# A token-mixing layer's twelve gate projections, moved among attention and into its preparation

## The chip, the cores and the metric

The program runs on one core of one Trainium2 chip. The metric is the device time of one execution, in microseconds (us), and less is better.

## The reference

The program computes two transformer blocks of two layers each, all in float32, on 256 tokens of width 1024. The first block (retention and state-space branches, and a feed-forward) isn't touched. The second block works on the first one's result `x` and on a context `ctx` of 256 tokens. Its mixing, for each layer, is:

```python
z = h @ lp["w_in"]
cq, ckv, kr, zf, zp, zg = jnp.split(z, SPLITS, axis=-1)
q = _mla_q(cq, lp, ang)
k, v = _mla_kv(ckv, kr, lp, ang)
att = _latent_attention(q, k, v, kv_ctx)      # 8 heads, 512 keys: the context's 256 and x's 256
y_a = att @ lp["w_oa"]
y_b = _fourier_mix(zf) @ lp["w_ob"]
y_c = _pool_mix(zp, lp["w_grp"], lp["pool_scale"]) @ lp["w_oc"]
g = jax.nn.sigmoid(zg + lp["b_gate"])         # 3 gates of width 1024
g_a, g_b, g_c = jnp.split(g, 3, axis=-1)
return (g_a * y_a + g_b * y_b + g_c * y_c) @ lp["w_out"], (k, v)
```

Behind it, each layer has a part in which every token gathers 128 rows of a table (the "peer" part). The mixing runs three times: once for the context (layer 0), and twice for `x` (layers 0 and 1).

## The kernel before

A planner (`Plan`) writes one list of items by hand, and each engine's program goes through that list in its order and issues its own part of each item. So the list fixes the order on every engine, and an engine that waits holds all that stands behind it. Two generators are merged into the list: `x_stream` (the first block, then for each layer `mix_phase` and `peer_x`) and `context_stream` (the context's mixing and its peer part). A step that yields `"alone"` writes out what is left of the context stream before the list goes on.

The mixing is `mixer`. Its items for `x`, in their order:

- the preparation: `keys_values` in three steps (`low_rank` projection with `wkv` and `key_roped`; `low_turn`, which transposes the normalised rows on TensorE and scales them on VectorE at L1988; `kv_up` with `wukv`, L1561 and L1565), between its first two steps `low_rank` of the queries with `wcq`, then `low_turn` of the queries (transposes at L1333), and four `q_up` (96 rows at L1298, then the rotation at L1579).
- the attention: `attend` has 18 steps. Step i issues `att_out` of pair i-2 (products 64 wide at L1298), `att_turnp` of pair i-1 (transposes at L1333, which wait for ScalarE's exponential at L2402) and `att_score` of pair i (L1586). After eight heads an `att_turn` follows.
- `spectral`: the two items `fourier` and `pool`.
- twelve gates, `token_gate`: each is a product of a 1 MB weight `wzg` with `hT`, 16 products of 256 columns at L1298 (the trace has 32 records for them), and two tanh on ScalarE (L2421).
- four `mix`, each of three gates with the three branches, and four `token_out` with `wout`.

`beside(a, na, b, nb)` interleaves two generators evenly by their step counts. For `x` in layer 1 (`wide`) the two spectral items and the twelve gates stand beside the 18 attention steps, since twelve gate buffers have room there. For `x` in layer 0 only the two spectral items stand there, and the gates come behind attention, three ahead of each `mix`, in three buffers that lie on the preparation's memory. Weights are loaded through a ring of five 1 MB slots (`self.wx`) by SyncE's queue in the items' order: a load waits until the slot's last reader is done, and later loads stand behind it. PSUM banks are taken in rotation out of six.

Of the kernel before, what the change touches and what calls it, by code (L numbers as in the profile page):

```python
# [130 lines left out]
BIG_N = 53208  # L131
# [3 lines left out]
class Plan:  # L135
# [47 lines left out]
    def tick(self, name, by=1):  # L183

        self.counts[name] = self.counts.get(name, 0) + by
        return (self.sem(name), self.counts[name])

    def put(self, kind, **args):
        self.items.append((kind, args))
# [67 lines left out]

    def x_stream(self, ar):
        yield from self.first_block()
        for l in range(2):  # L260
            ar.at = self.xmark
            yield from self.mix_phase(self.px, Ring(self.wx), self.small, ar, l, self.X, 0, True)
            side = Arena(self.big, BIG_N - SIDE, SIDE)
            yield from self.peer_x(self.px, self.small, self.A0 + self.xmark, BIG_N - self.A0 - self.xmark - SIDE, l,
                                   self.X, iter(()) if l else self.context_keys(),
                                   [side.get(2048) for _ in range(3 if l else 4)], side if l else None)
# [554 lines left out]
    def mixer(self, banks, wr, sm, ar, l, hT, hT_ok, X, vec, rope_on, cs):  # L821
        put, tick, t = self.put, self.tick, self.t
# [3 lines left out]
            K, Vv = self.KC, self.VC  # L826
        attT = ar.get(1024, (4, 256))
        early = rope_on
        wide = rope_on and l == 1

        def mixed_buffers():
            return [ar.get(1024 if i == 1 else 512, (2, 512 if i == 1 else 256)) for i in range(6)]

        if early:
            zfT, AB, fT, zp, poT, pyT = mixed_buffers()
        sg_slots = [Slot(ar.get(512, (2, 256))) for _ in range(12)] if wide else None
        mark = ar.at
        kv = self.keys_values(banks, wr, sm, ar, l, hT, hT_ok, K, Vv, cs)
        yield next(kv)
        cqn, cqT = ar.get(512, (2, 256)), ar.get(512, (2, 256))  # L840
# [5 lines left out]
        w = self.load(wr, t["wcq"][l], 2048)  # L846
        made, scaled = self.low_rank(banks, sm, [w], w.ap.rearrange("p (k n) -> p k n", k=8), hT, None, 256, cqn)
        w.free(made)
        yield
        kv_ok = yield from kv  # L850
        if rope_on and l == 1:
            kv_ok += self.ctx_kv_ok
        turned = self.low_turn(banks, sm, 256, cqn, cqT, self.col[l, "qg"], scaled)
        yield 2
        w = self.load(wr, t["wuq"][l], 1536)
        wq = w.ap[:, 0:1536].rearrange("p (k n) -> p k n", k=2)
        for h in range(0, 8, 2):
            u = banks.take()
# [4 lines left out]
        w.free(u.full)  # L863

        nk = 4 if rope_on else 2
        got = {}

        def attend():
            state = {}
            pairs = [self.KC, K] if rope_on else [K]  # L870
            vals = [self.VC[:, 0, :], self.VC[:, 1, :]] + ([Vv[:, 0, :], Vv[:, 1, :]] if rope_on else [])
            if not rope_on:
                vals = [Vv[:, 0, :], Vv[:, 1, :]]
            for i in range(18):
                if i >= 2:
                    tt, h = divmod(i - 2, 8)
                    c, rc, pt, pt_ok = state.pop(i - 2)
                    u = banks.take()
                    pt.free(u.full)
                    put("att_out", pt=pt, vals=vals, h=h, nk=nk, u=u, ready=pt_ok, rc=rc, sm=sm, c=c,  # L880
                        dst=att[:, tt, 64 * h:64 * h + 64])
                    got["used", i - 2] = u.free
                    if h == 7:
                        ut = banks.take()
                        put("att_turn", src=att[:, tt, :], dst=attT[:, :, tt * P:tt * P + P], u=ut, ready=u.free)
                        got["aT"] = ut.free
                if 1 <= i < 17:
                    c, rc, p, e_ok = state.pop(i - 1)
                    pt, u = pts.take(), banks.take()
                    put("att_turnp", p=p, nk=nk, u=u, pt=pt, ready=e_ok)  # L890
                    p.free(u.full)
                    state[i - 1] = (c, rc, pt, u.free)
                if i < 16:
                    tt, h = divmod(i, 8)
                    u, p, c = banks.take(), prs.take(), 16 + 4 * (i % 4)
                    rc = tick("att_recip")
                    put("att_score", q=Q[:, h, tt * P:tt * P + P], pairs=pairs, h=h, nk=nk, u=u, p=p, sm=sm, c=c, rc=rc,
                        peak=tick("att_peak"), ready=[q_ok, *kv_ok] if i == 0 else [], before=got.get(("used", i - 4)))
                    state[i] = (c, rc, p, u.free)
                yield  # L900

        def spectral():
            w, u = self.load(wr, t["wzf"][l], 2048), banks.take()
            w.free(u.full)
            w2, ua = self.load(wr, t["dft"], 2048), [banks.take() for _ in range(2)]
            uf = banks.take()
            w2.free(uf.full)
            put("fourier", ws=[w, w2], u=u, ua=ua, uf=uf, hT=hT, zfT=zfT, AB=AB, fT=fT)
            got["f_ok"] = uf.free
            yield  # L910
            w, u = self.load(wr, t["wzp"][l], 2048), banks.take()
            w.free(u.full)
            w2, up = self.load(wr, t["pool"], 2048), banks.take()
            w2.free(up.full)
            w3, ug = self.load(wr, t["wgrp"][l], 256), banks.take()
            w3.free(ug.full)
            put("pool", ws=[w, w2, w3], u=u, up=up, ug=ug, hT=hT, zp=zp, poT=poT, pyT=pyT, psc=self.col[l, "psc"])
            got["py_ok"] = ug.free
            yield

        def gate(b, c, s):
            w, u = self.load(wr, t["wzg"][l, b, c], 2048), banks.take()
            w.free(u.full)
            n = 8 * b + 2 * c
            put("token_gate", ws=[w], u=u, hT=hT, s=s, bias=[self.col[l, "bg"][:, n + m:n + m + 1] for m in range(2)])
            return s, u.free

        def spectral_and_gates():
            yield from spectral()
            for c in range(4):  # L930
                for b in range(3):
                    got["gate", c, b] = gate(b, c, Turn(sg_slots[3 * c + b]))
                    yield

        if wide:
            yield from self.beside(spectral_and_gates(), 14, attend(), 18)
        elif early:
            yield from self.beside(spectral(), 2, attend(), 18)
        else:
            yield from attend()  # L940
        if not wide:
            ar.at = mark
            if not early:
                zfT, AB, fT, zp, poT, pyT = mixed_buffers()
                yield from spectral()
            sg_slots = [Slot(ar.get(512, (2, 256))) for _ in range(3)]
# [5 lines left out]
        for c in range(4):  # L952
            sgs = []
            for b in range(3):
                if wide:
                    sgs.append(got["gate", c, b])
                else:
                    sgs.append(gate(b, c, Turn(sg_slots[b])))
                    yield
            w, us = self.load(wr, t["woabc"][l, c], 2048), [banks.take() for _ in range(3)]  # L960
            w.free(us[2].full)
            for (s, _), u in zip(sgs, us):
                s.free(u.free)
            mixed = tick("mixed")
            put("mix", ws=[w], us=us, srcs=((attT, 0, 4), (fT, 4, 2), (pyT, 6, 2)), sgs=sgs, ty=ty,
                MT=MT[:, 2 * c:2 * c + 2, :], done=mixed, ready=[got["aT"], got["f_ok"], got["py_ok"]] if c == 0 else [])
            yield
        m2_ok = tick("d_m2_c" if vec else "d_m2_x", 16)
        put("load_row", dst=m2, src=self.mods[l, vec, 2:3, :].to_broadcast([P, 1024]), done=m2_ok, before=[got["aT"]])
        for i in range(4):  # L970
            w, u = self.load(wr, t["wout"][l, i], 2048), banks.take()
# [1758 lines left out]
```

## Time and profile before

| | us |
|---|---|
| median of 3 runs | 4190.04 (4188.73 to 4191.44) |
| the profiled execution | 4178.77 |
| its span | 4177.5 |
| mixing of `x` in layer 0, from the query projection to the output projection | 238.13 |
| the same in layer 1 | 217.21 |

The profiled execution was 11.27 us shorter than the median of the runs. The two stretches go from the start of the query `low_rank` on TensorE to the start of the first `token_out`; the work of TensorE in them is the same.

### The profile page before, as it was taken

To read this page: it belongs to the slowest core of one execution; us is meant where nothing else is said; L and a number is where in the kernel's file an instruction comes from. 1 tells how busy PE (TensorE), PEld (TensorE's weight loads), DVE (VectorE), ACT (ScalarE), POOL (GpSimd) and SP (SyncE) were. 2 spreads that over 40 slices of the span, in tenths; PEclk is the share of its full clock that TensorE was granted. 3 is DMA by queue.
4 is the path that set the end of the run, shared out by engine and by line. 5 is a ranking of instruction groups with operands and counts; after the bars stand their busy time and mean duration, and the time that the engine had idled before them with its cause. 6 is when DMAs were issued, how large, how long until landed. Compare 5 with 4: busy or idle time off the path is not lost. (4 is left out here: it accounts for less than half of the span.)

```text
span 4177.5 us, 41027 instructions
## 1 busy us (share of the span) xinstructions
PE 3664.8 (88%) x14584; PEld 2586.0 (62%) x14584; DVE 2318.4 (55%) x5464; ACT 656.9 (16%) x1800; POOL 1291.4 (31%) x1125
## 2 busy tenths in 40 slices
PE   8988999998998889999897998777778998887777
PEld 6667788887846778888745874333334786433333
DVE  3432011557757896766742147766764126777875
ACT  2332001110001320000012111111112211111111
POOL 1100000000655566765620014434442002444442
PEclk9999999999999999999999999988999999999989
DMA  8742344334998889998961449988996237999998
GB/s 320 283 193 88 122 151 181 122 130 150 411 390 308 296 334 397 404 392 343 413 238 53 145 186 389 412 340 359 415 416 281 102 116 295 385 419 420 419 419 332
DMA packets 207818, 1208.65 MB, mean 289 GB/s; under 512 B 23696, under 2 KB 24848, under 8 KB 96000
## 3 DMA queue, kind: packets, MB, share of 16 engines
q0 software_dynamic: 154368, 855.71, 51.1%
q1 hardware_dynamic: 53248, 350.32, 22.1%
q8 instruction: 118, 1.93, 0.2%
q14 instruction: 84, 0.69, 0.0%
HBM read 1204.79 MB, written 1.15 MB: 289 GB/s over the span
## 5 line engine op out<-in xcount | busy, mean ns | idle before, releaser
L1298 PE MATMUL bank<-big 128*128 128x256 f32 (+5 forms) x9848 | 2140.5, 378 | 64.1 <-DVE big L1796 8.7
L1298 PEld LDWEIGHTS bank<-big 128*128 128x128 f32 (+2 forms) x9848 | 1833.9, 191 | 377.9 <-issue 72.5
L2489 POOL DMA_INDIRECT big<-in_pboth,big x1024 | 1227.9, 1199 | 1208.1 <-PE bank L1685 705.2
L1685 PE MATMUL bank<-big 128*128 128x512 f32 x2048 | 1000.0, 647 | 276.6 <-ACT big L2453 276.6
L2169 DVE CUSTOM_DVE_ANT_0 big<-big 128x1024 f32<-128x1024 f32 x768 | 926.1, 1223 | 326.0 <-DMA big<-in_pboth,big 323.1
L1685 PEld LDWEIGHTS bank<-big 128*128 128x128 f32 x2048 | 413.4, 207 | 854.3 <-issue 492.6
L2476 POOL TENSOR_TENSOR big<-big 128x1 f32<-128x1 f32 (+1 forms) x49 | 37.7, 770 | 1519.8 <-DVE big L1739 1519.8
L2180 DVE SCALAR_TENSOR_TENSOR big<-big 128x1024 f32<-128x1024 f32 x254 | 326.2, 1284 | 61.5 <-DMA big<-in_pboth,big 41.5
L2453 ACT ACTIVATE big<-big 128x128 f32<-128x128 f32 x512 | 164.9, 391 | 244.0 <-DVE big L2148 239.7
L1333 PE MATMUL bank<-big 128*128 128x128 f32 x596 | 94.9, 294 | 66.0 <-ACT big L2402 19.8
L2443 ACT ACTIVATE big<-big 128x4 f32<-128x4 f32 (+2 forms) x134 | 27.7, 207 | 727.5 <-DVE big L2144 727.4
L1488 PE MATMUL bank<-big 128*128 128x512 f32 x256 | 113.9, 607 | 21.2 <-DVE big L1903 21.2
L1333 PEld LDWEIGHTS bank<-big 128*128 128x128 f32 x596 | 74.0, 153 | 84.4 <-issue 39.4
L2047 DVE SCALAR_TENSOR_TENSOR big<-big,bank 128x512 f32<-128x512 f32 x36 | 24.8, 689 | 176.1 <-PE bank L1298 176.1
L2025 DVE TENSOR_REDUCE big<-bank 128x1 f32<-128x512 f32 (+1 forms) x48 | 28.9, 602 | 152.8 <-PE bank L1586 152.8
L1812 DVE SCALAR_TENSOR_TENSOR big<-big,bank 128x512 f32<-128x512 f32 x32 | 22.0, 687 | 148.0 <-ACT big L2281 148.0
L1488 PEld LDWEIGHTS bank<-big 128*128 128x128 f32 x256 | 49.6, 195 | 84.7 <-issue 62.7
L1889 DVE SCALAR_TENSOR_TENSOR big<-big,bank 128x256 f32<-128x256 f32 x32 | 13.4, 420 | 152.7 <-PE bank L1298 152.6
L1796 DVE SCALAR_TENSOR_TENSOR big<-bank,big 128x255 f32<-128x255 f32 (+1 forms) x144 | 62.7, 477 | 61.4 <-ACT big L2269 59.7
L2238 ACT ACTIVATE big<-big 128x1024 f32<-128x1024 f32 x26 | 27.4, 1055 | 403.0 <-DVE big L1909 168.1
L2421 ACT ACTIVATE big<-bank,big 128x256 f32<-128x256 f32 x72 | 30.2, 471 | 305.2 <-PE bank L1298 305.2
L2482 POOL DMA_DIRECT2D big<-in_wmod x48 | 25.8, 540 | 153.8 <-PE bank L1510 153.8
(203 smaller groups left out, 2177.0 us busy)
## 6 DMA issues: line engine op xcount, KB each, us to landing
big<-in_w SPq DMA_DIRECT2D x104, 1024.0 KB, 7.6
big<-in_wmod POOLq DMA_DIRECT2D x48, 1024.0 KB, 8.4
big<-in_wgu SPq DMA_DIRECT2D x44, 1024.0 KB, 8.0
big<-in_wzg SPq DMA_DIRECT2D x36, 1024.0 KB, 4.7
big<-in_wro SPq DMA_DIRECT2D x32, 1024.0 KB, 6.9
big<-in_wpq SPq DMA_DIRECT2D x24, 1024.0 KB, 6.1
big<-in_wd SPq DMA_DIRECT2D x22, 1024.0 KB, 8.1
big<-in_pboth,big POOLq DMA_INDIRECT x1024, 11.7
```

What stands on the lines that cost most here:

```text
L1298: last = pe.matmul(o, a, b, start=(i == 0), stop=(i == n - 1))
L1333: last = pe.transpose(o[:, i, :], b, ident)
L1488: last = pe.matmul(us[2 * tt + n].ap, act[:, 2 * i + k, tt * P:tt * P + P], wk[:, k, 512 * n:512 * n + 512], start=(i + k == 0), stop=False)
L1685: last = pe.matmul(u.ap, d.ap, row[:, 512 * i:512 * i + 512], start=(k == 0), stop=(k == 127))
L1796: i = v.scalar_tensor_tensor(c[:, m, s:256], o[:, m, 0:256 - s], conv["w"][m][:, 3 - s:4 - s], c[:, m, s:256], ALU.mult, ALU.add)
L2025: step(v.reduce_max(sm[:, c:c + 1], u.ap[:, 0:nk * P], AX.X))
L2169: v.tensor_tensor_reduce(row, row, h, 1.0, 0.0, ALU.mult, ALU.add, out).then_inc(done[0], 1)
L2180: v.scalar_tensor_tensor(at, s.ap, by, at, ALU.mult, ALU.add).then_inc(done[0], 1)
L2421: last = e.activation(sc.ap[:, m, :], by2(u.ap)[:, m, :], ACT.Tanh, scale=0.5, bias=bias[m])
L2453: s.activation(d.ap, p.ident, ACT.Copy, scale=by).then_inc(diag[0], 1)
L2476: g.tensor_tensor(r.sm[:, 8 + r.at:8 + r.at + r.n], r.sm[:, 4 + r.at:4 + r.at + r.n], r.sm[:, 12:13].to_broadcast([P, r.n]), ALU.pow).then ...
L2489: g.indirect_dma_start(out=s.ap, out_offset=None, in_=table, in_offset=bass.IndirectOffsetOnAxis(ap=index, axis=0)).then_inc(s.full[0], 16)
```

## The change

For `x`, layer 0 takes the shape of layer 1: twelve gate buffers, here in the context stream's memory (free once the context's last item, `c_ok`, is done), and the gates in the list beside attention. In both layers the first three gates now stand in the preparation: one ahead of the keys' `low_turn`, one between that and `kv_up`, one between the queries' `low_turn` and `q_up`. The two spectral items come next, and the nine other gates, beside the 18 steps. The context's mixing keeps its order. In the list of items nothing moves ahead of the mixing of `x`: the context stream has already ended there, so that the new `"alone"` moves none of them.

```diff
     def x_stream(self, ar):
         yield from self.first_block()
+        yield "alone"
...
-        wide = rope_on and l == 1
+        wide = rope_on
...
-        sg_slots = [Slot(ar.get(512, (2, 256))) for _ in range(12)] if wide else None
+        if wide:
+            far = ar if l else Arena(self.big, self.B0, BIG_N - self.B0)
+            sg_slots = [Slot(far.get(512, (2, 256))) for _ in range(12)]
+            for s in sg_slots:
+                s.freed = self.c_ok
...
+        def spectral_and_gates():
+            for c in range(4):
+                for b in range(3):
+                    got["gate", c, b] = gate(b, c, Turn(sg_slots[3 * c + b]))
+                    yield
+                if c == 0:
+                    yield from spectral()
...
         yield
+        got = {}
+        fill = spectral_and_gates() if wide else iter(())
+        next(fill, None)
+        yield next(kv)
+        next(fill, None)
         kv_ok = yield from kv
...
         turned = self.low_turn(banks, sm, 256, cqn, cqT, self.col[l, "qg"], scaled)
+        next(fill, None)
         yield 2
...
-        def spectral_and_gates():
-            yield from spectral()
-            for c in range(4):
-                for b in range(3):
-                    got["gate", c, b] = gate(b, c, Turn(sg_slots[3 * c + b]))
-                    yield
-
         if wide:
-            yield from self.beside(spectral_and_gates(), 14, attend(), 18)
-        elif early:
-            yield from self.beside(spectral(), 2, attend(), 18)
+            yield from self.beside(fill, 11, attend(), 18)
         else:
             yield from attend()
```

The order on TensorE in the preparation, from the queries' `low_rank` (16 products of 256 columns) to the first `q_up` (96 wide). Before:

```order
L1298 MATMUL bank<-big 128x256 x16
L1333 MATMUL bank<-big 128x128 x2
L1561 MATMUL bank<-big 64x256 x8
L1565 MATMUL bank<-big 128x512 x2
L1333 MATMUL bank<-big 128x128 x4
L1298 MATMUL bank<-big 96x256 x4
```

And now (line numbers are higher by 10 in the changed kernel):

```order
L1308 MATMUL bank<-big 128x256 x32
L1343 MATMUL bank<-big 128x128 x2
L1308 MATMUL bank<-big 128x256 x16
L1571 MATMUL bank<-big 64x256 x8
L1575 MATMUL bank<-big 128x512 x2
L1343 MATMUL bank<-big 128x128 x4
L1308 MATMUL bank<-big 128x256 x16
L1308 MATMUL bank<-big 96x256 x4
```

Three gates (16 products of 256 columns each) have come in: one behind `low_rank` and one behind each of the two groups of transposes. Both layers have these rows.

The order on TensorE in layer 1's attention, from the end of `pool` (L1638) on; a step is `att_out` (64 wide), transposes, `att_score` (L1586). Before:

```order
L1638 MATMUL bank<-big 128x256 x2
L1298 MATMUL bank<-big 128x64 x4
L1333 MATMUL bank<-big 128x128 x4
L1586 MATMUL bank<-big 128x256 x2
L1298 MATMUL bank<-big 128x256 x16
L1298 MATMUL bank<-big 128x64 x4
L1333 MATMUL bank<-big 128x128 x4
L1586 MATMUL bank<-big 128x256 x2
L1298 MATMUL bank<-big 128x256 x16
L1298 MATMUL bank<-big 128x64 x4
L1333 MATMUL bank<-big 128x128 x4
L1586 MATMUL bank<-big 128x256 x2
```

And now, in both layers:

```order
L1648 MATMUL bank<-big 128x256 x2
L1308 MATMUL bank<-big 128x64 x4
L1343 MATMUL bank<-big 128x128 x4
L1596 MATMUL bank<-big 128x256 x2
L1308 MATMUL bank<-big 128x64 x4
L1343 MATMUL bank<-big 128x128 x4
L1596 MATMUL bank<-big 128x256 x2
L1308 MATMUL bank<-big 128x256 x16
L1308 MATMUL bank<-big 128x64 x4
L1343 MATMUL bank<-big 128x128 x4
L1596 MATMUL bank<-big 128x256 x2
L1308 MATMUL bank<-big 128x64 x4
```

Of the first steps behind `pool`, layer 1 had a gate ahead of each; now the third step has none, the fourth has one and the fifth has none. In steps 3 to 15 ten gates stood before in layer 1 and seven stand now.

The end of layer 0's mixing on TensorE before, from the last attention steps to the output projection (20 groups of 16: twelve gates, four `mix`, four `token_out`):

```order
L1298 MATMUL bank<-big 128x64 x4
L1333 MATMUL bank<-big 128x128 x4
L1298 MATMUL bank<-big 128x256 x320
L1343 MATMUL bank<-big 128x256 x10
```

And now:

```order
L1308 MATMUL bank<-big 128x64 x4
L1343 MATMUL bank<-big 128x128 x4
L1308 MATMUL bank<-big 128x256 x128
L1353 MATMUL bank<-big 128x256 x10
```

The twelve gates have left this place (192 products).

## Rows read from the trace of the kernel before

**Rows 1.** The core's span and granted TensorE clock.

```profile
core 0: 4177.5 us, clock 0.951
```

**Rows 2.** Windows of both mixings of x: length, busy us by engine, clock, DMA.

```profile
core 0: us, PE busy (x) PEld busy (x) DVE busy (x) ACT busy (x) POOL busy (x), PEclk, DMA share, GB/s
2188.70:2426.80 238.10, 210.60 (x983) 171.90 (x981) 44.39 (x94) 46.69 (x108) 0.70 (x1) 0.95 0.29 104
3216.20:3433.50 217.30, 200.21 (x984) 166.55 (x983) 44.37 (x94) 47.58 (x108) 0.69 (x1) 0.98 0.32 114
```

**Rows 3.** TensorE's timeline, starts of query projection and output projection: start, us, work, [idle].

```profile
2188.70 7.10 PE L1298 MATMUL bank<-big 128*128 128x256 f32 x32
...
2426.83 28.00 PE L1298 MATMUL bank<-big 128*128 128x256 f32 x128 [1.60 <-DVE big L2052]
...
3216.25 7.10 PE L1298 MATMUL bank<-big 128*128 128x256 f32 x32
...
3433.46 28.00 PE L1298 MATMUL bank<-big 128*128 128x256 f32 x128 [1.61 <-DVE big L2052]
```

**Rows 4.** TensorE's timeline, layer 1's preparation.

```profile
3223.19 0.38 PE L1333 MATMUL bank<-big 128*128 128x128 f32 x2
3224.99 3.67 PE L1561 MATMUL bank<-big 128*64 128x256 f32 x16 [1.43 <-DVE big L1988]
...
3230.41 0.60 PE L1333 MATMUL bank<-big 128*128 128x128 f32 x4
3232.11 1.94 PE L1298 MATMUL bank<-big 128*96 128x256 f32 x8 [1.10 <-DVE big L1988]
...
3245.52 1.07 PE L1579 MATMUL bank<-big 96*96 96x512 f32 x2 [0.76 <-ACT big L2381]
3248.90 2.05 PE L1586 MATMUL bank<-big 96*128 96x256 f32 x4 [2.31 <-issue]
```

**Rows 5.** TensorE's timeline, layer 1's attention.

```profile
3283.01 1.03 PE L1586 MATMUL bank<-big 96*128 96x256 f32 x4
...
3292.09 1.03 PE L1586 MATMUL bank<-big 96*128 96x256 f32 x4
...
3331.92 1.03 PE L1586 MATMUL bank<-big 96*128 96x256 f32 x4
...
3335.16 1.06 PE L1333 MATMUL bank<-big 128*128 128x128 f32 x8 [1.17 <-ACT big L2386]
3336.06 1.03 PE L1586 MATMUL bank<-big 96*128 96x256 f32 x4
...
3384.97 1.03 PE L1586 MATMUL bank<-big 96*128 96x256 f32 x4
...
3402.54 0.63 PE L1333 MATMUL bank<-big 128*128 128x128 f32 x4 [0.56 <-ACT big L2386]
```

**Rows 6.** TensorE's timeline, layer 0: two attention steps without a gate, gates and mix.

```profile
2259.49 0.63 PE L1333 MATMUL bank<-big 128*128 128x128 f32 x4 [0.97 <-ACT big L2402]
...
2262.99 0.63 PE L1333 MATMUL bank<-big 128*128 128x128 f32 x4 [0.97 <-ACT big L2402]
...
2329.73 95.50 PE L1298 MATMUL bank<-big 128*128 128x256 f32 x440
```

**Rows 7.** Windows at the start of attention: layer 0, layer 0 further on, layer 1.

```profile
2219.00:2241.00 22.00, 17.13 (x54) 14.10 (x54) 6.01 (x15) 5.38 (x13) 0.00 (x0) 0.54 0.00 0
2241.00:2286.00 45.00, 35.44 (x197) 27.67 (x197) 9.45 (x26) 15.12 (x37) 0.00 (x0) 1.00 0.14 48
3247.00:3255.00 8.00, 6.10 (x14) 4.90 (x15) 2.71 (x6) 0.78 (x2) 0.00 (x0) 0.57 0.00 0
```

**Rows 8.** DMA issues of layer 1's mixing: count, KB each, median us to landing.

```profile
big<-in_wzg SPq DMA_DIRECT2D x6, 1024.0 KB, 4.8
...
big<-in_wzf SPq DMA_DIRECT2D x1, 1024.0 KB, 10.9
```

**Rows 9.** Timeline: the context's last addition on VectorE; a gate's tanh pair on ScalarE.

```profile
2139.59 2.36 DVE L2202 TENSOR_TENSOR big<-big 128x1024 f32<-128x1024 f32 x2
...
3291.01 0.84 ACT L2421 ACTIVATE big<-bank,big 128x256 f32<-128x256 f32 x2 [5.18 <-PE bank L1298]
```

More of the change, by code:

```diff
@@ L835, in mixer, with spectral, gate @@
             zfT, AB, fT, zp, poT, pyT = mixed_buffers()
-        sg_slots = [Slot(ar.get(512, (2, 256))) for _ in range(12)] if wide else None
-        mark = ar.at
+        if wide:
[3 more added lines that the diff above has]
+                s.freed = self.c_ok
+        mark = ar.at
+        def spectral():
+            w, u = self.load(wr, t["wzf"][l], 2048), banks.take()
+            w.free(u.full)
+            w2, ua = self.load(wr, t["dft"], 2048), [banks.take() for _ in range(2)]
+            uf = banks.take()
+            w2.free(uf.full)
+            put("fourier", ws=[w, w2], u=u, ua=ua, uf=uf, hT=hT, zfT=zfT, AB=AB, fT=fT)
+            got["f_ok"] = uf.free
+            yield
+            w, u = self.load(wr, t["wzp"][l], 2048), banks.take()
+            w.free(u.full)
+            w2, up = self.load(wr, t["pool"], 2048), banks.take()
+            w2.free(up.full)
+            w3, ug = self.load(wr, t["wgrp"][l], 256), banks.take()
+            w3.free(ug.full)
+            put("pool", ws=[w, w2, w3], u=u, up=up, ug=ug, hT=hT, zp=zp, poT=poT, pyT=pyT, psc=self.col[l, "psc"])
+            got["py_ok"] = ug.free
+            yield
+        def gate(b, c, s):
+            w, u = self.load(wr, t["wzg"][l, b, c], 2048), banks.take()
+            w.free(u.full)
+            n = 8 * b + 2 * c
+            put("token_gate", ws=[w], u=u, hT=hT, s=s, bias=[self.col[l, "bg"][:, n + m:n + m + 1] for m in range(2)])
+            return s, u.free
+        def spectral_and_gates():
+            for c in range(4):
+                for b in range(3):
+                    got["gate", c, b] = gate(b, c, Turn(sg_slots[3 * c + b]))
+                    yield
+                if c == 0:
+                    yield from spectral()
         kv = self.keys_values(banks, wr, sm, ar, l, hT, hT_ok, K, Vv, cs)
@@ L865, in mixer @@
         nk = 4 if rope_on else 2
-        got = {}
         def attend():
@@ L900, in attend @@
                 yield
[L902 to L909, printed above, removed]
-            yield
[L911 to L926, printed above, removed]
-        def spectral_and_gates():
-            yield from spectral()
-            for c in range(4):
-                for b in range(3):
-                    got["gate", c, b] = gate(b, c, Turn(sg_slots[3 * c + b]))
-                    yield
         if wide:
-            yield from self.beside(spectral_and_gates(), 14, attend(), 18)
-        elif early:
-            yield from self.beside(spectral(), 2, attend(), 18)
+            yield from self.beside(fill, 11, attend(), 18)
         else:
             yield from attend()
+        if not wide or l == 0:
+            ar.at = mark
         if not wide:
-            ar.at = mark
             if not early:
```

## The prediction

> **What bounds the kernel now.** I first read the windows over both mixings of `x` [rows 2]. TensorE is busy for 210.60 of 238.10 us in layer 0 and 200.21 of 217.30 in layer 1, ScalarE and VectorE under 48 each, the DMA queues at 0.29 and 0.32. TensorE sets the time here (its clock is granted at 0.951 over the whole span of 4177.5 us [rows 1]); what can be gained is its idle time and its time at the low clock. Both stretches hold the same work. By the starts of query and output projection [rows 3], layer 0 takes 2426.83 - 2188.70 = 238.13 us and layer 1 3433.46 - 3216.25 = 217.21. So the two orders of the gates have already run side by side in one execution, and the order of layer 1 is 20.92 us shorter.
>
> Where these 20.92 us lie: a gate in a dense stream costs 32 x 95.50/440 = 6.95 us [rows 6] wherever there is no gap to fill. An attention step without a gate repeats every 2262.99 - 2259.49 = 3.50 us: its transposes wait 0.97 us for the exponential [rows 6]. A step with a gate takes 3292.09 - 3283.01 = 9.08 us [rows 5]. So a gate put into a step costs 9.08 - 3.50 = 5.58, which is 1.37 less than in the stream (0.97 of wait and 0.4 of the pipe's draining and refilling). Ten or eleven gates covering such a gap give about 14 us. The rest is the clock: layer 0's attention starts with 22 us at a mean of 0.54 of the full 2.4 GHz, that is 20.2 us at 1.2 GHz; layer 1 shows 0.57 over 8 us, that is 6.9 us [rows 7]. Half of the difference is 6.7 us. 14 + 6.7 is close to 20.92, so I hold the difference explained.
>
> **The change, term by term.**
>
> *Layer 0 takes layer 1's old order*: -20.92 us, as measured between the layers. The stretch has the same dependences, the same ring and the same weights in both; only the bank numbers and the place of the buffers differ.
>
> *Three gates enter the preparation, in both layers.* They add 3 x 6.95 = 20.85 us there. The first stands ahead of the keys' transposes, which follow the query projection without any idle time (3216.25 + 7.10, next start 3223.19) [rows 3, 4]: it covers nothing. The second stands between those two transposes and `kv_up`. From 3223.19 to 3224.99 is 1.80 us, of which two transposes in a stream take 0.22 (four take some 0.45); 1.58 us go. The third stands between the queries' four transposes and `q_up`: 3232.11 - 3230.41 = 1.70, less 0.45, gives 1.25 us. The idle times alone, 1.43 and 1.10, would give 2.53, my lower bound for what is covered; I take 1.58 + 1.25 = 2.83, since the drain is covered as well. Net +18.02. The gaps of 0.76 between the four `q_up` and of 2.31 ahead of the first score [rows 4] stay.
>
> *The same gates leave the attention.* In steps 3 to 15 the old layer 1 has ten gates and three steps without one, of which one is the step with `att_turn`, 3336.06 - 3331.92 = 4.14 us [rows 5]: 10 x 9.08 + 2 x 3.50 + 4.14 = 101.94, and the trace has 3384.97 - 3283.01 = 101.96. By the new order there are seven gates and six plain steps, and one of the gates now stands in the step with `att_turn`. That combination is not in the trace at that place. I price it as 9.08 + 0.45 for four more transposes + 0.56 idle as where `att_turn` follows a gate at the end of attention [rows 5] + 0.17 of overlap lost in that wait = 10.26 (bounds 9.53, no wait, and 10.7, the full 1.17 of the row at 3335.16). So 6 x 9.08 + 10.26 + 6 x 3.50 = 85.74, which is 16.22 less. The two last steps keep their gates.
>
> *Sum of the moved three*: +18.02 - 16.22 = +1.80 us in each layer: taken out of the attention they saved 5.58 each, in the preparation they cost 6.95 each, less only two small gaps. With the bounds 2.53 and 3.2 for the gaps, and those of the `att_turn` step, it is +0.7 to +2.6. Layer 0: -20.92 + 1.80 = -19.12. Layer 1: +1.80. Together -17.3.
>
> *What could wait instead.* Loads: a gate's weight lands 4.8 us after its issue when it is alone, and the last of five issued together after 10.9 [rows 8]. Of the first five loads now three are the two gates' and `wukv` instead of `wukv`, `wuq` and `wzf`, about 4 MB either way; the first gate's product starts some 24 us after the issue. `wuq` has to wait for the slot of `wcq`, free when the query projection ends, and is needed three gates (20.8 us) and `kv_up` later; `wzf`, `dft`, `wzp` and `pool` follow in the queue as the gates and `kv_up` release their slots, each over 14 us ahead of its use. All are covered by TensorE's own products; without that cover each would cost up to 4.8 us. ScalarE: each gate puts 0.84 us of tanh [rows 9] ahead of the copies of K or Q. The first of four heads' K takes TensorE about as long, and the first `q_up` 1.94 us [rows 4]: nothing shows, at most 0.84 a gate. The gate buffers of layer 0 wait on ScalarE for the context's last item, which ended at 2141.95 [rows 9]; the first tanh stands at about 2188.70 + 14 = 2203, 61 us later.
>
> **The clock** is what I cannot price from one row. In both layers it falls to 1.2 GHz around the 2.31 us of idle that follow four `q_up` with gaps between them, and comes back inside `fourier` [rows 4, 7]. In layer 1 this costs about 6.9/2, less the idle part, some 3 us. The change leaves this sequence as it is, so I leave the 3 us in both layers. The Trainium skill says, in "TensorE: Matmul & The Clock Gate" (Part 1: The HAM clock gate), that the low clock is the default and that activity releases it; by that a denser preparation may hold the clock, and the sum would be up to 6 us lower. The trace agrees so far that the falls come with idle time; whether the gates ahead of `q_up` are enough no row shows.
>
> **Sum.** The profiled execution would go from 4178.77 to 4161.5 us. It stood 11.27 us under the median of the runs; I see nothing in the mixings that explains it, so I put the same -17.3 on the median: 4190.04 - 17.3 = 4172.7 us.
>
> **Rivals.**
>
> 1. *The sum holds* (layer 0 like layer 1, the clock's fall as in layer 1): 4172.7, own range 4170 to 4176. Chance 0.63. For it: the two orders lie in one trace, and every other stretch keeps its order.
> 2. *The clock doesn't fall at the start of attention*, in one layer or both, because the third gate stands just ahead of `q_up`: 3 or 6 us less, 4169.7 or 4166.7. Against it: the idle stretch itself, 2.31 us behind thin work, is unchanged. Chance 0.20.
> 3. *The clock stays low for longer*, as in layer 0 before (20.2 us instead of 6.9 at 1.2 GHz, 6.7 us a layer): 4179. For it: six plain steps instead of three with idle time in each; against it: a row of plain steps of layer 0 ran at 1.00 [rows 7]. Chance 0.06.
> 4. *The change doesn't shorten the program*, as layer 0's mixing isn't what the rest waits for: the peer part behind it would start no earlier, and the time stays at 4190 to 4194. Against it: the output projection follows its work with 1.60 us of idle only [rows 3], and everything of the peer part starts from its result. Chance 0.06.
> 5. *Slower*: the tanh of the first gate is behind the context's last item on ScalarE, and all of ScalarE behind that tanh. If the context stream ended late, layer 0's whole preparation would stall. It decides from a delay of 61 us on, where the wait begins, and at 61 + 17 = 78 us nothing is left; at 90 us later the kernel would take about 4202. The rows show the context done 61 us ahead, and nothing that the change moves lies ahead of it. Chance 0.03.
>
> A remainder of 0.02 is for what I don't see.
>
> **Numbers.** A measurement of this kernel can tell about 0.2%, 8.4 us, from no change. Rivals 1 to 3 all lie more than that below 4190.04: with the margin of the sum, 0.91 for faster, 0.06 for no difference, 0.03 for slower. The range of 8 in 10 takes in rivals 1 and 2 whole and most of 3: 4165 to 4179.
>
> **What would show it.** In the profile of the changed kernel: from query projection to output projection, now with one gate more ahead of the keys' transposes, both layers about 219 us. No idle ahead of `kv_up` and the first `q_up`. Six plain steps with 0.97 us of idle ahead of their transposes between steps 3 and 15, and a wait for L2386's counterpart of about 0.56 at the `att_turn` in the middle. The half clock for some 7 us at the start of each attention. I am wrong if the layers differ by more than 4 us, if a DMA or a bank appears among TensorE's waits of these stretches, or if a stretch outside the mixings changes its length by more than 2 us.

## The result and the profile after

| | before | after |
|---|---|---|
| median, us (7 runs each) | 4189.67 (4184.69 to 4192.37) | 4175.02 (4172.86 to 4179.59) |
| ratio, 95% interval | | 0.9967 (0.9956 to 0.9978) |
| the profiled execution, us | 4178.77 | 4172.86 |
| mixing of `x`, layer 0, us | 238.13 | 220.85 |
| mixing of `x`, layer 1, us | 217.21 | 217.58 |
| between the mixings, us | 789.42 | 794.65 |
| behind the second mixing, us | 744.04 | 750.24 |

The changed kernel is 14.65 us faster by the medians; the forecast was 17.3. The whole interval lies below 1, on the side of faster. The two mixings together became 17.28 - 0.37 = 16.91 us shorter. The two profiled executions differ by 5.91 us only, because the stretches outside the mixings, whose code did not change, were 11.4 us longer in the second one.

TensorE's timeline of the changed kernel in layer 1: start, length, line, work, [idle before, what ended it].

```profile
3203.78 14.03 PE L1308 MATMUL bank<-big 128*128 128x256 f32 x64
3217.65 0.38 PE L1343 MATMUL bank<-big 128*128 128x128 f32 x2
3217.87 7.10 PE L1308 MATMUL bank<-big 128*128 128x256 f32 x32
3224.90 3.67 PE L1571 MATMUL bank<-big 128*64 128x256 f32 x16
...
3230.32 0.60 PE L1343 MATMUL bank<-big 128*128 128x128 f32 x4
3230.75 8.83 PE L1308 MATMUL bank<-big 128*128 128x256 f32 x40
...
3254.43 1.83 PE L1596 MATMUL bank<-big 96*128 96x256 f32 x4 [2.32 <-issue]
3256.06 8.09 PE L1308 MATMUL bank<-big 128*128 128x256 f32 x32
...
3287.20 1.03 PE L1596 MATMUL bank<-big 96*128 96x256 f32 x4
...
3290.17 0.63 PE L1343 MATMUL bank<-big 128*128 128x128 f32 x4 [0.96 <-ACT big L2412]
...
3334.23 1.07 PE L1343 MATMUL bank<-big 128*128 128x128 f32 x8 [0.56 <-ACT big L2396]
...
3421.36 28.00 PE L1308 MATMUL bank<-big 128*128 128x256 f32 x128 [1.61 <-DVE big L2062]
```

The first row holds the query projection and a gate without a gap. The idle times of 1.43 and 1.10 us of [rows 4] are gone: `kv_up` (L1571) and the first `q_up` (the last 8 of the 40 records at 3230.75) follow a gate at once. The 2.32 us ahead of the first score have stayed. In the attention plain steps wait 0.96 or 0.97 us, and the step with `att_turn` (L1343 x8) waits 0.56 us instead of the 1.17 of [rows 5].

The same timeline in layer 0, around what layer 1 doesn't have:

```profile
2238.93 2.05 PE L1596 MATMUL bank<-big 96*128 96x256 f32 x4 [2.31 <-issue]
2240.77 8.84 PE L1308 MATMUL bank<-big 128*128 128x256 f32 x32
...
2285.18 1.03 PE L1596 MATMUL bank<-big 96*128 96x256 f32 x4
2286.17 1.08 PE L1308 MATMUL bank<-big 128*128 128x64 f32 x8
2288.56 0.99 PE L1343 MATMUL bank<-big 128*128 128x128 f32 x4 [1.32 <-ACT big L2412]
...
2409.13 28.00 PE L1308 MATMUL bank<-big 128*128 128x256 f32 x128 [1.61 <-DVE big L2062]
```

One plain step waits 1.32 us for the exponential instead of 0.97 (what was late is in the last section), and behind it four transposes take 0.99 us instead of 0.63. For these and for the long first rows the windows of the changed kernel tell why (length, busy by engine, then the granted clock, here 0.77, 0.76 and 0.87, and DMA):

```profile
2235.00:2250.00 15.00, 11.75 (x38) 8.87 (x38) 3.25 (x7) 1.53 (x4) 0.00 (x0) 0.77 0.03 9
2285.00:2292.00 7.00, 5.68 (x27) 4.65 (x25) 1.64 (x4) 2.47 (x7) 0.00 (x0) 0.76 0.45 153
3251.00:3264.00 13.00, 10.64 (x38) 8.16 (x38) 2.98 (x6) 0.78 (x2) 0.00 (x0) 0.87 0.03 10
```

TensorE ran at 1.2 GHz for 6.9 us at the start of layer 0's attention, for 3.4 us at the start of layer 1's, and once more for 3.4 us in layer 0 around that longer wait.

### The profile page after: what moved, and what is told of

The parts are those of the page before. It is cut to its first block and busy times, and to the rows that moved or that the text cites. A ratio compares the mean times of both kernels' runs of the same rounds, so it can differ in the third digit from the quotient of the medians.

```text
span 4171.6 us, 41042 instructions
## 1 busy us (share of the span) xinstructions
PE 3669.1 (88%) x14584; PEld 2587.9 (62%) x14584; DVE 2321.4 (56%) x5464; ACT 657.2 (16%) x1800; POOL 1283.5 (31%) x1125
## 5 line engine op out<-in xcount | busy, mean ns | idle before, releaser
L1343 PE MATMUL bank<-big 128*128 128x128 f32 x596 | 95.5, 296 | 64.0 <-ACT big L2310 20.6
L2035 DVE TENSOR_REDUCE big<-bank 128x1 f32<-128x512 f32 (+1 forms) x48 | 28.9, 603 | 173.6 <-PE bank L1596 173.6
L1343 PEld LDWEIGHTS bank<-big 128*128 128x128 f32 x596 | 75.0, 154 | 81.4 <-issue 35.0
```

The lines of the kernel that those rows point to most:

```text
L1343: last = pe.transpose(o[:, i, :], b, ident)
L2035: step(v.reduce_max(sm[:, c:c + 1], u.ap[:, 0:nk * P], AX.X))
```

## The experiments

All mixings below are cut at the same four points of TensorE's timeline: P, from the query projection to the first score; F, with `fourier` and `pool`, to the third score (step 2); S, the thirteen steps to the score of step 15; E, from there to the output projection. The table is worked out from the timeline of each profile, in us.

| kernel | layer | P | F | S | E | sum |
|---|---|---|---|---|---|---|
| before | 0 | 32.66 | | | | 238.13 |
| before | 1 | 32.65 | 34.11 | 101.96 | 48.49 | 217.21 |
| changed | 0 | 50.65 | 33.74 | 87.97 | 48.49 | 220.85 |
| changed | 1 | 50.65 | 32.77 | 85.67 | 48.49 | 217.58 |
| changed, third execution | 0 | 50.66 | 31.09 | 86.30 | 48.48 | 216.53 |
| shape_only | 0 | 32.65 | 34.16 | 102.32 | 48.48 | 217.61 |
| shape_only | 1 | 32.65 | 31.10 | 103.63 | 48.49 | 215.87 |
| two_gaps | 0 | 43.72 | 33.79 | 92.39 | 48.49 | 218.39 |
| two_gaps | 1 | 43.72 | 32.77 | 92.40 | 48.49 | 217.38 |
| behind_q_up | 0 | 48.18 | 31.02 | 86.30 | 48.48 | 213.98 |
| behind_q_up | 1 | 48.18 | 31.01 | 85.67 | 48.49 | 213.35 |
| one_behind_q_up | 0 | 37.12 | 31.02 | 96.84 | 48.49 | 213.47 |
| one_behind_q_up | 1 | 37.11 | 31.02 | 98.88 | 48.49 | 215.50 |
| gap_and_behind | 0, 1 | 42.55 | 31.02 | 90.72 | 48.49 | 212.78, 212.77 |
| q_up_staggered | 0 | 38.77 | 31.02 | 90.72 | 48.49 | 209.00 |
| q_up_staggered | 1 | 38.77 | 31.02 | 92.39 | 48.49 | 210.67 |

The second execution of the changed kernel repeats each cell of its two rows within 0.02 us. At full clock F is 31.02 us.

Theory 1 is that of the prediction: a product in the stream costs what it takes, one in a plain attention step 1.37 us less, the gain is layer 0's shape, and the three moved gates cost a little. Its rivals stand with each run. Every ratio is to the kernel before, measured beside the run on the same chip.

### Both kernels once more

> The kernel before, unchanged, for its profile alone. In the two profiles so far the stretch between the mixings (first output projection to the query projection of layer 1) went from 789.4 us before to 794.7 after, and the stretch behind the second mixing from 744.0 to 750.2, together 11.4 us longer, while the two mixings became 16.9 us shorter. Theory 1 (the profiled execution of before was a short one; the peer part varies by itself): here one or both stretches come out longer, 792 to 798 and 747 to 752, and the mixings at 238.1 and 217.2 as before within 2 us. Rival (the change lengthens the peer part): 789.4 and 744.0 again within 1.5 us.

> The changed kernel, unchanged. Mixing stretches 220.8 and 217.6 us again within 3 us (clock at the start of attention differs from execution to execution); ratio to before about 0.9967. Theory 1: the stretch between the mixings and the one behind differ from 794.7 and 750.2 by 1 to 5 us. Rival: they come out as 794.7 and 750.2 within 1.5.

Windows from output projection to the next query projection, and from the second output projection to the end: the kernel before, first execution, and below it the second one.

```profile
2426.80:3216.20 789.40, 628.29 (x1680) 314.64 (x1681) 522.81 (x1480) 133.03 (x419) 296.57 (x264) 0.93 0.89 362
3433.50:4177.50 744.00, 599.91 (x1508) 292.04 (x1508) 517.66 (x1454) 116.19 (x380) 284.83 (x260) 0.92 0.92 379
```

```profile
2427.20:3224.30 797.10, 643.41 (x1681) 321.43 (x1682) 523.20 (x1480) 133.19 (x419) 297.44 (x264) 0.91 0.89 359
3441.30:4189.50 748.20, 598.52 (x1508) 292.30 (x1508) 517.80 (x1454) 116.20 (x380) 287.92 (x260) 0.93 0.92 377
```

The same kernel took 797.1 and 748.2 us in its second profile, 11.9 more than in the first, with the same instructions to within a record; its mixings were 237.81 and 217.01. (TensorE was granted 0.91 instead of 0.93 and busy for 15.1 us more in the longer first stretch, but 0.93 instead of 0.92 in the second, which was longer too; why these stretches vary stays open.) That settles it for theory 1: the first profile of before was a short one. The changed kernel's repeat gave 797.27 and 749.04, and mixings of 220.83 and 217.59. In all 13 profiles the first stretch lies between 787.2 and 800.7 us and the second between 744.0 and 750.2; the kernel before has 789.4 and 797.0 in the first, the changed one 794.7, 797.3 and 794.8, so no effect of the gates' order can be told there. The repeat's median was 4169.85 us beside 4186.62 for the kernel before, its ratio 0.9955 (0.9942 to 0.9969).

### Layer 0's shape alone

The three `next(fill, None)` of the preparation are left out, and `spectral` comes ahead of the first gate:

```diff
+                    if 3 * c + b == 0:
+                        yield from spectral()
...
-                if c == 0:
-                    yield from spectral()
...
-        next(fill, None)
         yield next(kv)
-        next(fill, None)
         kv_ok = yield from kv
...
-        next(fill, None)
         yield 2
...
-            yield from self.beside(fill, 11, attend(), 18)
+            yield from self.beside(fill, 14, attend(), 18)
```

> Layer 0 in layer 1's old order (twelve buffers in the context's memory, all twelve gates beside attention), no gate in the preparation. Theory 1 (the gain is all from layer 0's shape, the three moved gates cost 1.8 us a layer): both mixings 217.2 us, the time 20.9 us under before (ratio 0.9950) and 3.6 under the changed kernel. Rival (the moved gates help): both mixings longer than in the changed kernel at equal clock, the time above the changed kernel's by 1 us or more.

The mixings were 217.61 and 215.87 us, together 4.95 less than in the changed kernel. The time was 4169.51 (ratio 0.9954, 0.9941 to 0.9968) beside 4169.85 for the changed kernel. The 3.6 us that were expected between them can't be told in whole times, where the five runs of each spread over more than 11 us. By the parts of the table, P is 18.00 shorter and S 16.29 longer (101.96 in before's layer 1 against 85.67), so the moved gates cost 1.71 us a layer; the rest is the clock and what comes with it. F also shows something unexpected. In layer 1 the clock did not fall at the first score, with no gate in the preparation at all:

```profile
3242.16 1.10 PE L1593 MATMUL bank<-big 96*128 96x256 f32 x4 [2.32 <-issue]
3243.10 7.10 PE L1305 MATMUL bank<-big 128*128 128x256 f32 x32
```

The 32 records of `fourier` take 7.10 us, at 2.4 GHz throughout. It fell at the `att_turn` step instead (S is 1.67 longer). So gates in the preparation are not needed for the clock to stay; behind the same idle time it falls in most executions and in some it doesn't.

### Without the gate that covers nothing

The `next(fill, None)` ahead of `yield next(kv)` is left out, and `spectral` comes after two gates.

> As the changed kernel, without the gate that covers nothing: only the two gates between transposes and kv_up and between transposes and q_up stand in the preparation, the third is beside attention again. Theory 1 (a gate costs 6.95 us outside attention's steps and 5.58 in one; the two gaps give 1.58 and 1.25): against all twelve beside attention 2 x 6.95 - 2.83 - 11.16 = -0.1 us, so no gain and no loss from the two, each mixing 217.1 us at the clock of layer 1 before, 1.9 under 219.0. Rival (every gate moved ahead costs alike): +1.2 against twelve beside attention.

The mixings took 218.39 and 217.38 us, not 217.1. P was 43.72 and S 92.40, so 11.07 more than without gates there and 9.56 less in S: the two moved gates cost 1.51 us, not -0.1. P fits (2 x 6.95 - 2.83 = 11.07). S was expected 11.16 less; the clock fell at `att_turn` in both layers (S is 1.68 longer than the 90.72 of gap_and_behind, which has the same order there). With 90.72 it is -0.17. So the size of theory 1 holds by the parts, not in the whole mixing, and its rival (+1.2) isn't excluded by the sum alone. The time was 4161.24 us (ratio 0.9955, 0.9940 to 0.9970).

### The third gate behind q_up

The first line below stands ahead of `yield next(kv)`, the second behind the loop over `q_up`.

```diff
-        next(fill, None)
...
+        next(fill, None)
```

> As the changed kernel, but the first of the three gates stands behind the last q_up, ahead of the first score, instead of ahead of the keys' transposes. Theory 1 (2.31 us of idle stand there, and the clock's fall comes from them): no idle ahead of the first score, the clock stays at 1.00 through fourier, each mixing 2.45 + 3 us shorter than 217.2 + 1.8, about 213.6 us; time some 10 us under the changed kernel. Rival (the clock falls because q_up itself is thin): the gap goes, but a half clock shows at the gate or fourier, each mixing about 216.5, time some 5 us under the changed kernel.

Measured 213.98 and 213.35 against 213.6. TensorE's timeline in layer 0, and the windows over the same place in both layers:

```profile
2225.97 1.07 PE L1589 MATMUL bank<-big 96*96 96x512 f32 x2 [0.76 <-ACT big L2391]
2226.88 7.10 PE L1308 MATMUL bank<-big 128*128 128x256 f32 x32
2233.82 1.03 PE L1596 MATMUL bank<-big 96*128 96x256 f32 x4
2234.68 7.10 PE L1308 MATMUL bank<-big 128*128 128x256 f32 x32
```

```profile
2225.00:2245.00 20.00, 18.51 (x77) 14.35 (x77) 4.17 (x8) 2.79 (x6) 0.00 (x0) 1.00 0.30 95
3233.00:3253.00 20.00, 18.51 (x79) 14.21 (x78) 4.08 (x9) 2.79 (x6) 0.00 (x0) 1.00 0.28 90
```

The idle time is gone, P is 2.47 us shorter, and the clock stays at 1.00 through `fourier`: theory 1. The time was 4161.85 us (ratio 0.9941, 0.9927 to 0.9954), 8.0 under the changed kernel's repeat.

### One gate, and two, with the last behind q_up

In the first, `next(fill, None)` stands behind `q_up` only; in the second, behind `q_up` and between the keys' transposes and `kv_up`. `spectral` follows behind these gates.

> One gate alone stands in the preparation, behind the last q_up. Theory 1: no idle ahead of the first score, clock at 1.00 through fourier. Four plain steps in attention, a gate in the step with att_turn. Each mixing 217.2 - 3.0 (clock) - 2.45 + 6.95 - 5.04 = 213.7 us. Rival (the clock held in the last run because of all three gates, the denser preparation): a half clock again at the first score or in fourier, about 216.7.

> Two gates in the preparation: between the keys' transposes and kv_up, and behind the last q_up. Theory 1: 217.2 - 3.0 - 1.58 - 2.45 + 2 x 6.95 - 11.16 = 212.9 us for each mixing, the shortest of the orders tried; the time some 12 us under the changed kernel's 219.0-based sum, within 2 us of the run with three. Rival: no shorter than the order with three (213.7).

> The order with two gates in the preparation (before kv_up, behind q_up) once more. Theory 1: mixings 212.8 and 212.8 us, or about 2 more where ScalarE's one late exponential in the attention brings the half clock; together 8 to 13 us under the changed kernel's, and the time so too. Rival (the 4146.85 was a lucky chip): within 4 us of the changed kernel.

With one gate layer 0 took 213.47 us (213.7 expected) and F was 31.02 in both layers: one gate at this place does what three did, so the rival (it takes the denser preparation to hold the clock) falls. Layer 1 took 2.03 more, from one late exponential (0.35) and a fall of the clock behind it. With two gates four mixings in two profiles took 212.77 or 212.78 us (212.9 expected). The times were 4156.89 (ratio 0.9946, 0.9933 to 0.9960) with one, 4146.85 (0.9933, 0.9917 to 0.9950) and 4149.14 (0.9937, 0.9924 to 0.9950) with two. Beside the latter the changed kernel ran once more on the same chip:

> The changed kernel once more, beside the next two on the same chip. Mixings 220.8 and 217.6 us within 3.

It took 4164.20 us (ratio 0.9961, 0.9948 to 0.9975), and its mixings 216.53 and 217.58. So the order with two gates was 15 us faster by the medians, more than the 8 to 13 expected; the mixings of the two profiles give 8.57, within what was expected of them, and nothing was changed outside.

### Layer 0 as before

```diff
-        wide = rope_on
+        wide = rope_on and l == 1
...
+        elif early:
+            yield from self.beside(spectral(), 2, attend(), 18)
```

> Layer 0 as in the kernel before (gates behind attention, three buffers); layer 1 as in the changed kernel. Theory 1 (the gain is layer 0's shape): mixings 238 and 217.5 to 219 us, the time that of before within 0.2%. Rival (the three gates in the preparation give part of the gain): layer 1 well under 217, the time 5 us or more under before.

The mixings were 236.87 and 217.58 us, and the time 4181.58 us (ratio 1.0003, 0.9994 to 1.0013). So without layer 0's new shape there is no gain, and the rival's 5 us lie outside the interval.

### The rotations of q_up behind the next product

Here only TensorE's program differs from gap_and_behind: each rotation is held back until the next `q_up` has issued its product.

```diff
+    def turn_q(u, u2, Q):
+        opened(u2)
+        pe.wait_ge(*u.free)
+        pe.matmul(by2(u2.ap[0:96, :]), p.pmat, Q, start=True, stop=True).then_inc(u2.full[0], 1)
...
         if u2:
-            opened(u2)
-            pe.wait_ge(*u.free)
-            pe.matmul(by2(u2.ap[0:96, :]), p.pmat, Q, start=True, stop=True).then_inc(u2.full[0], 1)
+            if h:
+                turn_q(*held.pop())
+            held.append((u, u2, Q))
+            if h == 6:
+                turn_q(*held.pop())
```

> As gap_and_behind, and on TensorE each q_up's rotation stands behind the product of the next two heads, so that ScalarE's copy is covered. Theory 1 (the 0.76 us of idle and some 0.2 of drain go three times): each mixing 212.8 - 2.8 = 210.0 us. Rival (VectorE's rotation, three operations of 0.69 us and their waits, is then the bound of the stretch): 211.5 or more, with TensorE waiting at its end.

P went from 42.55 to 38.77, 3.78 instead of 2.8 us less: the last rotation, too, no longer waits for its copy.

```profile
2209.76 3.68 PE L1307 MATMUL bank<-big 128*96 128x256 f32 x16 [1.10 <-DVE big L2006]
2213.27 1.02 PE L1581 MATMUL bank<-big 96*96 96x512 f32 x2
2214.13 1.89 PE L1307 MATMUL bank<-big 128*96 128x256 f32 x8
2215.86 1.02 PE L1581 MATMUL bank<-big 96*96 96x512 f32 x2
2216.72 1.90 PE L1307 MATMUL bank<-big 128*96 128x256 f32 x8
2218.45 2.00 PE L1581 MATMUL bank<-big 96*96 96x512 f32 x4
2220.29 7.10 PE L1307 MATMUL bank<-big 128*128 128x256 f32 x32
```

The stretch has no idle row from the first product to the gate, so the rival (VectorE as its bound, with TensorE waiting at the end) did not come. Layer 0's mixing took 209.00 us; layer 1's took 210.67, with a fall of the clock at `att_turn` (S 1.67 longer). The time was 4145.66 us (ratio 0.9920, 0.9908 to 0.9933), whose interval lies clear of the kernel before and of the changed one (0.9948 to 0.9975). Against gap_and_behind (4149.14 beside it) the intervals overlap: the gain of 3.78 us in each P is shown by the timelines alone.

## Why the prediction was right

*Layer 0 takes layer 1's old order* (-20.92). shape_only has it alone: 217.61 us in layer 0, 20.5 less than 238.13; the rest is a late exponential of 0.35. layer1_only, without it, keeps the time of before. The split of the 20.92 into about 14 us of covered waits and 6.7 of clock was never tested by itself. It also left out a second stretch at 1.2 GHz in the old layer 0, behind the attention (from 2310 to 2318 us the mean is 0.79, that is 3.4 us), so the clock's part is up to 1.7 us larger. The term did not hang on this, since it was taken as measured.

*Three gates enter the preparation* (+18.02). P went from 32.65 to 50.65: +18.00. By the differences of P between the runs, the gate ahead of `kv_up` covered 6.95 - (42.55 - 37.12) = 1.52 us (1.58 expected), the one ahead of `q_up` 6.95 - (48.18 - 42.55) = 1.32 (1.25), and the first one 6.95 - (50.65 - 43.72) = 0.02. So the gaps gave more than their idle rows of 1.43 and 1.10 show; the bound of 3.2 for both had no row. Nothing else waited there: no DMA and no bank stands among the rows of TensorE, as expected.

*The same gates leave the attention* (-16.22). S went from 101.96 to 85.67 in layer 1: -16.29. The step with `att_turn` behind a gate, priced at 10.26 from rows of another place, took 10.26 from score to score in layer 1 (10.54 in layer 0). Its last part, 0.17 of lost overlap, had no row, so that it met the hundredth is luck.

*The sum* was 219.0 us for each mixing. Layer 1 took 217.58, for F was 1.34 shorter: the half clock lasted 3.4 us instead of 6.9. Layer 0 took 220.85, 1.84 more: F 0.37 less, and S 2.3 more than layer 1's for one late exponential (0.35), a fall of the clock behind it, and 0.27 at `att_turn`. Here the step failed that reads "I leave the 3 us in both layers". The mechanism was right, but the cost is no constant: in the profiles it is between 0 and 3.1 us at the first score (F from 31.1 to 34.2), and a second fall can come inside the attention. That one layer came out 1.84 over and the other 1.42 under, so that the sum of both was met within 0.4 us, is luck. In the third execution's layer 0, without either fall, the mixing took 216.53. Rival 2 came true there, but not by its mechanism, the gate ahead of `q_up`: shape_only has no such gate and shows the same in its layer 1.

*Outside the mixings* I had said that I was wrong if a stretch changed its length by more than 2 us. It did, by 5.2 and 6.2 us, and the second profile of before shows that this bound was too narrow: the kernel before varies by 7.6 and 4.2 there itself. That also covers the 11.27 us which I could not explain, by which the first profiled execution stood under the median. It was right to put the difference on the median and not the sum on the profile.

Rivals 4 and 5 did not come: the output projection and all behind it moved with the mixing, and the first tanh (at 2202.41 us) waited for TensorE's product, not for the context. Nor did rival 3: after `fourier` the clock is back, in every profile with layer 1's order. What it said of plain steps came in part: later falls of 3.4 us each, in the attention.

## What to carry to other kernels

Price independent work by where it is put, not by how much there is of it: in this kernel an independent product gave back the idle time that it covered and 0.1 to 0.4 us more, and cost its full length everywhere else. The first gate stood where nothing waited, two stood in gaps worth 1.5 and 1.3 us, and all three had been worth 1.37 each where they came from; the largest idle time of the stretch, 2.3 us, was left, and one gate there gave 2.5 us and kept the clock up. And compare stretches whose code moved, not whole executions: here the unchanged stretches vary by more than most of the steps.

## What was not expected of the hardware

- Behind 2.3 us of idle, which follow four `q_up` with idle time between them, the granted clock fell to 1.2 GHz before `fourier` ended in 11 of 13 mixings in which `fourier` follows the first score, and not in the two others (F of 31.09 and 31.10). With a gate in that place it fell in none of ten (F of 31.01 or 31.02 in each). That an activity monitor decides this is what the Trainium skill says, in "TensorE: Matmul & The Clock Gate" (Part 1: The HAM clock gate). The granted clock agrees so far as these falls come with idle time; why the same rows bring one in one execution and none in another no run here shows. It also fell behind single waits in the attention: in 3 of 6 mixings with a wait of 1.32 us, and, with layer 1's order, in 4 of the 12 with a plain step at `att_turn`, whose wait is 1.17 or 1.18.
- One exponential in each attention starts 0.35 us late, and the delay is VectorE's, not ScalarE's. The changed kernel's second execution, layer 0, has the score on TensorE, the maximum over it on VectorE (L2035) and the exponential on ScalarE (L2412); first the late one, below it one without a delay.

```profile
2287.95 1.03 PE L1596 MATMUL bank<-big 96*128 96x256 f32 x4
2289.44 0.69 DVE L2035 TENSOR_REDUCE big<-bank 128x1 f32<-128x512 f32 x1 [7.55 <-PE bank L1596]
2290.41 0.69 ACT L2412 ACTIVATE big<-bank,big 128x512 f32<-128x512 f32 x1 [1.62 <-DVE big L2037]
...
2315.13 1.03 PE L1596 MATMUL bank<-big 96*128 96x256 f32 x4
2316.27 0.69 DVE L2035 TENSOR_REDUCE big<-bank 128x1 f32<-128x512 f32 x1 [1.55 <-PE bank L1596]
2317.24 0.69 ACT L2412 ACTIVATE big<-bank,big 128x512 f32<-128x512 f32 x1 [1.27 <-DVE big L2037]
```

  From score to maximum it is 1.49 us instead of 1.14, from maximum to exponential 0.97 both times. The place is fixed: step 4 in layer 0 and step 6 in layer 1, in all 23 mixings with layer 1's order. It costs time only where the next step has no gate (layer 0 in the changed kernel, shape_only and behind_q_up, layer 1 in one_behind_q_up). The order with two gates has a gate in both places, which is why its mixings never showed it. Counted from 0, the late maxima are always the records 2879 and 4671 of the 6369 that VectorE has in each trace, seven times 256 apart. Three more a multiple of 256 away (2111, 4159, 5439) start equally late in all 13 profiles, 0.40 us behind the end of their waits, though they are other instructions; in layer 0's old order record 2879 is a reciprocal, and is not late. So the delay goes by the place in VectorE's program; its cause stays open, and no run was made for it. The 0.27 us at `att_turn` in layer 0 come from ScalarE: its activation L2396 starts 0.28 us late there with nothing that it waits for. What matters most is what follows a late exponential: a fall of the clock, in two of the changed kernel's three profiles, for 1.7 us.
